# A transformer kernel of two blocks: attention probabilities turned on VectorE and through DRAM instead of on TensorE

## The chip, the cores and the metric

One NeuronCore of a Trainium2 chip runs the whole program. The metric is the time of one execution in device microseconds, taken as the median of three runs. A core has TensorE (matrix products into PSUM), VectorE (DVE in the profile), ScalarE (ACT), GpSimd (POOL), the sync engine (SP), whose queue issues nearly all DMAs here, and 16 DMA engines. All data is float32; products of the large weights are made of three products of rounded parts (fp32r).

## The reference

A sequence of 256 positions with 1024 features goes through two layers. The change is in the second one, in its "forgetting attention": 16 heads of 64 features, causal, in blocks of 128 queries, with a bias of cumulated gate logarithms. Its output is gated with that of another branch.

```
def forgetting_attention(q, k, v, f_pre, q_g, k_g):
    ...
    F = jnp.moveaxis(jnp.cumsum(jax.nn.log_sigmoid(f_pre.astype(f32)), axis=1), 1, 2)
    ...
        logits = jnp.einsum('bhqd,bhkd->bhqk', q_blk, k).astype(f32) * scale + (F_blk[..., :, None] - F[..., None, :])
        logits = jnp.where(k_pos[None, :] <= q_pos[:, None], logits, -jnp.inf)
        p = jax.nn.softmax(logits, axis=-1)
        return jnp.einsum('bhqk,bhkd->bhqd', p.astype(v.dtype), v)
    ...
    merged = jax.nn.sigmoid(g_a) * (y_a @ w_branch_a) + jax.nn.sigmoid(g_b) * (y_b @ w_branch_b)
    x = x + g2 * (merged @ w_out)
```

For the last product TensorE needs the probabilities with the keys on the partitions, while the softmax leaves them with the queries on the partitions: each 128x128 block must be turned.

## The kernel before, in words

The layers are a row of large products (blocks), each of units of two 128-row slices of a weight and 512 columns. A unit is loaded by SP into one of four raw buffers, rounded by ScalarE (`whi`, L1595), and VectorE makes the remainder (`wlo`, L1983). TensorE then runs a half unit for each of the two tiles of 128 positions: six matmuls of 512 columns (L1319, L1323, L1324). The prepared halves stand in five buffers, six from the second branch product on.

Everything else is fitted between the half units. A planner (`plan`, from the top of `build`) writes one list, `order`, which all engines follow. Each side job is a generator that puts its next segment into the list and yields a number of ticks; the numbers are in the table `LAG`. One tick passes behind a half unit, but several in the blocks of `PACED`: `("pace", "gb0")` is 4, `("pace", "gb1")` 9. A call of `drain` lets ticks pass without half units, so that the side jobs stand densely there. Every engine takes its own part of a segment, in the order of the list, and waits on semaphores.

Around the change the blocks are o0, o1 (output gate), ga0, ga1 (gate of branch a), then a drain until `yT` (the turned output of the first branch) is done, then ba0, ba1 (branch product a), gb0, gb1, a drain, bb0, bb1. The jobs of the attention are, for each half of the heads (`fx0`, `fx1`, eight heads each):

- `job_scores`: four rounds. In each, TensorE makes the scores of four heads (L1414), VectorE scales them and adds the bias NF into a buffer of P (L2205, 256 keys for the late queries, 128 for the early ones, which come second), and ScalarE takes the exponential (L1754). P_f is a ring of three buffers of 512 columns.
- `job_weigh`: for i = 0 to 7 (two heads each) TensorE transposes four or two 128x128 blocks of P into a PSUM bank (L1439). VectorE (even i, L2247) or ScalarE (odd i, L1777) copies them to PT_f, a ring of two. One step later TensorE weighs the values with them, PT as stationary operand, fV with 64 columns as moving one (L1458). Each of these float32 products is two records in the trace. After i = 3 and i = 7 VectorE divides the bank by the sums of the exponentials into W1 (L2262, L2267). For `fx0` the end of the first such group waits until `yT` is done, since W1 still holds its input.

Another way of turning is in use elsewhere in the kernel: VectorE turns all 32x32 blocks of a tile in place (L2344, L2509), SP stores the result to the scratch tensor `scr_u` in DRAM (L2713, L2731) and fetches it in another order (L2719, L2738), which puts the blocks where a full transposition has them. The FFN's hidden units (tiles `blocked`, `land_m`, `land_f`) and the queries and keys of this attention (`gate`, which is `gates[0]`, and `land_h`) go that way. `land_h` takes the place of the two buffers PT_f, which are used later. The row `gates[1]` is loaded for the residual behind this stage (`gate_row(1)`).

## Time and profile before

| | |
|---|---|
| median of 3 runs | 945.15 us (944.30 to 945.33) |
| profiled execution, its own time | 944.73 us |
| its span in the trace | 943.4 us |
| TensorE matmuls, busy | 935.1 us, 99% |
| TensorE weight loads, busy | 772.3 us, 82% |
| VectorE, busy | 718.6 us, 76% |
| ScalarE, busy | 509.9 us, 54% |
| granted TensorE clock | 0.999 |
| moved by DMA | 240.31 MB, 255 GB/s on average |

The page gives for each engine the time in which it ran an instruction, and the same in slices of the span. Matmuls are pipelined and their ends are modelled: a duration of 390 ns stands for a matmul that is followed by the next after 230. The distance between starts, or the chain of waits, which charges each piece with the time until the next, tells what a matmul costs. A wait is counted only where an engine had nothing to do, and is put down to what released it.

### The profile page before, as it was taken

How to read it: one execution, taken by the hardware profiler on the slowest of the kernel's cores; microseconds unless marked ns; L12 is line 12 of the kernel's file. 1: busy time of each engine (PE TensorE's matmuls, PEld its weight loads, DVE VectorE, ACT ScalarE, POOL GpSimd, SP SyncE). 2: the span in 40 equal slices, each digit the busy share in tenths (PEclk: the TensorE clock that was granted, in tenths of full speed). 3: DMA queues.
4: the chain of work that ended last, by engine and by line, in shares of the span. 5: the costliest groups of instructions: out<-in, count | busy, mean ns of one | idle time of the engine just before them, and what ended most of it. 6: DMA issues, size and time to landing. Idle time of an engine off the chain costs nothing.

```text
span 943.4 us, 12244 instructions
## 1 busy us (share of the span) xinstructions
PE 935.1 (99%) x4426; PEld 772.3 (82%) x4426; DVE 718.6 (76%) x1090; ACT 509.9 (54%) x792; POOL 50.1 (5%) x58
## 2 busy tenths in 40 slices
PE   9999999999999999999999999999999999999998
PEld 7878788888887888888888888878788888888886
DVE  6897689998676888777769999788666765566662
ACT  6686665564446445454576565456464574544440
POOL 2410000000000000000000121110000000000000
PEclk9999999999999999999999999999999999999999
DMA  9840779999894989998747889984735647666870
GB/s 341 266 152 23 246 245 372 389 387 371 286 317 148 332 326 343 320 345 299 274 133 259 279 281 283 302 338 147 234 125 188 213 137 264 225 223 223 300 234 23
DMA packets 123130, 240.31 MB, mean 255 GB/s; under 512 B 9346, under 2 KB 28954, under 8 KB 122814
## 3 DMA queue, kind: packets, MB, share of 16 engines
q1 hardware_dynamic: 122926, 239.27, 73.8%
q8 instruction: 35, 0.57, 0.2%
q10 hardware_dynamic: 144, 0.27, 0.1%
q14 instruction: 25, 0.20, 0.1%
HBM read 226.35 MB, written 14.20 MB: 255 GB/s over the span
## 4 chain that ended last, share of the span: by engine, by line
PE 87%; DVE 5%; DMA 5%; ACT 1%; issue 1%; SPq 1%; POOL 0%; DVEq 0%; ACTq 0%
PE ps L1319 27%; PE ps L1324 26%; PE ps L1323 26%; DMA raw<-in_w_mix 2%; DVE wlo L1983 2%; PE ps L1458 2%; PE ps L1414 1%; PE ps L1439 1%; PE ps L1350 1%; DMA land_h<-scr_u 1%; PE ps L1372 1%; ACT whi L1595 1%; DMA raw<-in_w_up 1%; DMA raw<-in_w_in 1%; PE ps L1571 1%
## 5 line engine op out<-in xcount | busy, mean ns | idle before, releaser
L1595 ACT ACTIVATE whi<-raw 128x1024 fp32r<-128x1024 f32 (+1 forms) x285 | 294.5, 1046 | 272.6 <-PE ps L1324 169.5
L1983 DVE TENSOR_TENSOR wlo<-raw,whi 128x1024 fp32r<-128x1024 f32 (+1 forms) x285 | 338.4, 1203 | 106.3 <-ACT whi L1595 105.8
L1319 PE MATMUL ps<-whi,hTh 128*128 128x512 f32 (+1 forms) x760 | 300.0, 395 | 0.2 <-DVE nat L2129 0.2
L1324 PE MATMUL ps<-whi,hTl 128*128 128x512 f32 (+1 forms) x760 | 294.4, 387 | 0.0
L1323 PE MATMUL ps<-wlo,hTh 128*128 128x512 f32 (+1 forms) x760 | 294.3, 387 | 0.0
L1319 PEld LDWEIGHTS ps<-whi,hTh 128*128 128x128 f32 x760 | 142.9, 188 | 30.8 <-issue 2.5
L1324 PEld LDWEIGHTS ps<-whi,hTl 128*128 128x128 f32 x760 | 142.7, 188 | 29.5
L1323 PEld LDWEIGHTS ps<-wlo,hTh 128*128 128x128 f32 x760 | 142.9, 188 | 27.8
L2325 DVE CUSTOM_DVE_ANT_0 araw<-araw,crow,colp 128x1024 f32<-128x1024 f32 x72 | 91.9, 1277 | 0.1
L2594 POOL TENSOR_TENSOR stat<-stat,mhalf 128x8 f32<-128x8 f32 (+3 forms) x29 | 36.2, 1260 | 586.0 <-DVE stat L1999 460.3
L1319 PE MATMUL ps<-whi,uh_ffn 128*128 128x512 f32 x164 | 63.9, 390 | 0.0
L1324 PE MATMUL ps<-whi,ul_ffn 128*128 128x512 f32 x164 | 63.8, 389 | 0.0
L1323 PE MATMUL ps<-wlo,uh_ffn 128*128 128x512 f32 x164 | 63.8, 389 | 0.0
L1319 PE MATMUL ps<-whi,uh 128*128 128x512 f32 x128 | 49.9, 390 | 0.0
L1323 PE MATMUL ps<-wlo,uh 128*128 128x512 f32 x128 | 49.8, 389 | 0.0
L1324 PE MATMUL ps<-whi,ul 128*128 128x512 f32 x128 | 49.8, 389 | 0.0
L2374 DVE TENSOR_TENSOR nat<-ps,nat 128x512 f32<-128x512 f32 (+1 forms) x24 | 15.4, 646 | 29.7 <-PE ps L1324 22.3
L1319 PEld LDWEIGHTS ps<-whi,uh_ffn 128*128 128x128 f32 x164 | 30.8, 188 | 6.4
L1324 PEld LDWEIGHTS ps<-whi,ul_ffn 128*128 128x128 f32 x164 | 30.8, 188 | 6.4
L1323 PEld LDWEIGHTS ps<-wlo,uh_ffn 128*128 128x128 f32 x164 | 30.8, 188 | 6.3
L1324 PEld LDWEIGHTS ps<-whi,ul 128*128 128x128 f32 x128 | 24.0, 188 | 5.0
L1323 PEld LDWEIGHTS ps<-wlo,uh 128*128 128x128 f32 x128 | 24.0, 188 | 5.0
(276 smaller groups left out, 1129.2 us busy)
## 6 DMA issues: line engine op xcount, KB each, us to landing
raw<-in_ffn_w_in SPq DMA_DIRECT2D x80, 512.0 KB, 5.1
araw<-in_w_mod SPq DMA_DIRECT2D x72, 512.0 KB, 5.6
raw<-in_w_mix SPq DMA_DIRECT2D x64, 512.0 KB, 4.9
raw<-in_ffn_w_out SPq DMA_DIRECT2D x44, 512.0 KB, 4.9
raw<-in_w_up SPq DMA_DIRECT2D x32, 512.0 KB, 5.4
raw<-in_w_down SPq DMA_DIRECT2D x32, 512.0 KB, 5.3
scr_u<-blocked SPq DMA_DIRECT2D x18, 512.0 KB, 5.0
raw<-in_w_out SPq DMA_DIRECT2D x16, 512.0 KB, 4.3
```

What stands on the lines that cost most here:

```text
L1319: pe.e.matmul(o, ah, h[:, j, :], start=s0, stop=False, skip_group_check=True)
L1323: pe.e.matmul(o, ah, l[:, j, :], start=False, stop=False, skip_group_check=True)
L1324: r = pe.e.matmul(o, al, h[:, j, :], start=False, stop=s1, skip_group_check=True)
L1350: r = pe.e.transpose(bank[:, c * 128:(c + 1) * 128], src[:, (4 * p + c) * 128:(4 * p + c + 1) * 128], ident[:, :])
L1372: r = pe.e.transpose(bank[:, c * 256 + t * 128:c * 256 + t * 128 + 128], src[t][:, (2 * p + c) * 128:(2 * p + c + 1) * 128], ident[:, :])
L1414: return pe.e.matmul(bank[:, c * w:(c + 1) * w], Q[rows, hp + c, ts], K[rows, kc(c), 0:w], start=True, stop=True)
L1458: r = pe.e.matmul(ob[:, h * 64:(h + 1) * 64], buf[:, (nk * c + k) * 128:(nk * c + k + 1) * 128], (fV if a["fox"] else VA)[:, k, v0:v0 + 64 ...
L1595: act.e.activation(uflat(whi, u), uflat(raw, u), ACT.Copy).then_inc(hi.up(u), 1)
L1983: v.tensor_tensor(uflat(wlo, u), uflat(raw, u), uflat(whi, u).bitcast(f32), SUB).then_inc(lo_dve.up(u), 1)
L2325: v.tensor_tensor_reduce(out=w, in0=w, in1=crow[:, :], scale=1.0, scalar=col("bada", 8 * m + i), op0=MUL, op1=ADD, accum_out=to).then_inc( ...
L2374: v.tensor_tensor(b[:, 0:n], pair_of(key)[t][:, c:512], b[:, 0:n], MUL).then_inc(glu.up(name, t), 1)
L2594: g.tensor_tensor(o, a, mhalf[:, 0:n], ALU.pow).then_inc(rstd.up(*key), 1)
```

## The change

The probabilities of `fx0` and `fx1` are no longer transposed by TensorE. For i = 0 to 3 (four heads each, two buffers of P) `swap` has VectorE transpose the 32x32 blocks of two P buffers into `gates[1]` (`blocked_p`). SP stores it to `scr_u` and fetches it into `land_h` (`shuttle_p`), 1024 columns each for i = 0, 1 and 512 for i = 2, 3. `weigh_blocks` weighs straight from `land_h` with a strided view as stationary operand. There is one buffer before the store and one behind the fetch: a swap waits for the store before it, a fetch for the weighing before it. P becomes a ring of four, two of P_f and two halves of `gates[0]`. VectorE waits ahead of the first scores for the jobs that used these buffers. The copies to PT_f and the PSUM banks for the turned blocks go. The lags of the jobs around are set anew, and the pace of gb1 goes from 9 to 6.

The table of lags, as far as it concerns this attention and the blocks beside it:

```
-       ("fox", "fetch"): 6, ("fox", "put"): 4, ("gate", "ga0"): 15, ("gate", "ga1"): 24, ("gate", "gb0"): 8,
-       ("gate", "gb1"): 11, ("fox", 0): 2, ("fox", 1): 5, ("fox", 2): 5, ("fx0", "wait"): 15, ("fx0s", "round"): 15,
...
+       ("fox", "turn"): 3, ("fox", "fetch"): 6, ("fox", "put"): 4, ("gate", "ga0"): 18, ("gate", "ga1"): 22,
+       ("gate", "gb0"): 16, ("gate", "gb1"): 22, ("fox", 0): 2, ("fox", 1): 5, ("fox", 2): 5, ("fx0", "wait"): 11,
+       ("fx0s", "round"): 15, ("fx0s", "wait"): 9, ("fx0s", 0): 1, ("fx0s", 1): 11, ("fx0s", 2): 30, ("fx0s", 3): 1,
+       ("fx0t", 0): 1, ("fx0t", 1): 11, ("fx0t", 2): 10, ("fx0t", 3): 1, ("fx0w", 0): 2, ("fx0w", 1): 1,
+       ("fx0w", 2): 1, ("fx0w", 3): 11, ("fx1", "wait"): 0, ("fx1s", "round"): 10, ("fx1s", "wait"): 0,
+       ("fx1s", 0): 10, ("fx1s", 1): 5, ("fx1s", 2): 5, ("fx1s", 3): 22, ("fx1t", 0): 1, ("fx1t", 1): 1,
+       ("fx1t", 2): 5, ("fx1t", 3): 11, ("fx1w", 0): 4, ("fx1w", 1): 1, ("fx1w", 2): 2, ("fx1w", 3): 3,
...
+       ("pace", "gb1"): 6, ("pace", "kb"): 1, ("pace", "ob0"): 6, ("pace", "ob1"): 16, ("pace", "qa"): 11,
...
+       ("vb", 0): 2, ("yT", "turn"): 35, ("yb", "turn"): 19, ("yb", "wait"): 10, ("fx0f", 0): 10, ("fx0f", 1): 1,
+       ("fx0f", 2): 6, ("fx0f", 3): 6, ("fx1f", 0): 9, ("fx1f", 1): 8, ("fx1f", 2): 8, ("fx1f", 3): 8}
```

`t` is the lag behind a swap, `w` behind a weighing, `f` behind a fetch. The buffers, the planner's new job and the parts of the engines:

```
-    PT_f = Ring([sb(f"fPT{i}", [128, 512], c=sM) for i in range(2)])
+    land_h = Ring([sb("land_h", [128, 1024], c=sM)])
...
+    blocked_h, blocked_p = Ring([gates[0]]), Ring([gates[1]])
+    P_x = Ring([P_f.bufs[0], P_f.bufs[1], gates[0][:, 0:512], gates[0][:, 512:1024]])
...
+        def job_weigh_blocks(name, ready):
...
+            for i in range(5):
+                if i < 4:
+                    while not {(name, 2 * i), (name, 2 * i + 1)} <= done or None not in blocked_p.held:
+                        yield 1
+                    blocked_p.take(name, i)
...
+                    seg(name)
+                    blocked_p.drop(name, i)
+                    yield lag(f"{name}t", i, 2)
+                if i:
+                    b, last = (i - 1) // 2, i % 2 == 0
+                    while not last and outs() >= OUTS or last and name == "fx0" and "yT" not in done:
+                        yield 1
...
+                    seg(name)
+                    land_h.drop(name, i - 1)
...
+                    yield lag(f"{name}w", i - 1, 2)
+                if i < 4:
+                    while None not in land_h.held:
+                        yield 1
+                    land_h.take(name, i)
+                    seg(name)
+                    yield lag(f"{name}f", i, 6)
```

```
+    def p_columns(name, i):
+        return 512 * attention(name)["chunks"](2 * i) // 2
...
+            def weigh_blocks(i):
+                nk = a["qt"](2 * i) + 1
+                ob = misc.buf(name, "o", i // 2)
+                by_key = land_h.buf(name, i)[:, 0:p_columns(name, i)].rearrange("p (m u k) -> p u k m", m=128, u=2)
...
+                pe.wait_ge(*ld_p(name, i))
...
+                            r = pe.e.matmul(ob[:, h * 64:(h + 1) * 64], by_key[:, u, nk * c + k], fV[:, k, v0:v0 + 64],
+                                            start=(k == 0), stop=(k == nk - 1))
+                r.then_inc(weighed.up(name, i), 1)
+                land_h.give(weighed(name, i), name, i)
...
+                if name == "fx0":
+                    dve.wait_ge(*m_summed(3, 1))
+                    dve.wait_ge(*h_sq(3, 1))
+                    dve.wait_ge(*st_h("fox3"))
...
+            def swap(i):
+                out = blocked_p.buf(name, i)[:, 0:p_columns(name, i)].rearrange("p (g i u k) -> p u g k i", g=4, u=2, i=32)
+                dve.wait_ge(*blocked_p.free(name, i))
+                for u in range(2):
+                    n = 2 * i + u
+                    dve.wait_ge(*p_exp(name, n))
+                    v.transpose(out[:, u], P.buf(name, n)[:, 0:p_columns(name, i) // 2].rearrange(
+                        "p (k j g) -> p g k j", j=32, g=4)).then_inc(swapped.up(name, n), 1)
+                    P.give(swapped(name, n), name, n)
...
+        def shuttle_p(name):
+            for i in range(5):
+                if i < 4:
+                    r, slot_at = p_columns(name, i), i % 2 * 131072
+                    sp.wait_ge(*swapped(name, 2 * i + 1))
+                    q.dma_start(bass.AP(scrU.tensor, slot_at, [[r, 128], [1, r]]), blocked_p.buf(name, i)[:, 0:r]).then_inc(
+                        st_p.up(name, i), 16)
+                    blocked_p.give(st_p(name, i), name, i)
+                    yield
+                if i:
+                    yield
+                if i < 4:
+                    sp.wait_ge(*st_p(name, i))
+                    sp.wait_ge(*land_h.free(name, i))
+                    q.dma_start(land_h.buf(name, i)[:, 0:r].rearrange("p (a x) -> p a x", a=4),
+                                bass.AP(scrU.tensor, slot_at, [[r // 4, 128], [32 * r, 4], [1, r // 4]])).then_inc(
+                                    ld_p.up(name, i), 16)
+                    yield
...
+            if g == 1:
+                sp.wait_ge(*st_p("fx1", 3))
```

## Rows read from the trace of the kernel before

**Rows 1.** The page: busy time of the engines over the whole span.

```profile
PE 935.1 (99%) x4426; PEld 772.3 (82%) x4426; DVE 718.6 (76%) x1090; ACT 509.9 (54%) x792; POOL 50.1 (5%) x58
```

**Rows 2.** Busy time by stage, 626 to 712 us; last columns granted clock, DMA share, GB/s.

```profile
626.00:646.00 20.00, 19.40 (x102) 15.55 (x103) 19.73 (x38) 14.40 (x33) 2.91 (x2) 1.00 0.69 236
646.00:661.00 15.00, 14.99 (x98) 12.89 (x97) 12.09 (x27) 9.48 (x21) 0.00 (x0) 1.00 0.31 105
661.00:677.00 16.00, 16.00 (x80) 12.82 (x80) 10.46 (x18) 8.34 (x15) 0.00 (x0) 1.00 0.71 225
677.00:712.00 35.00, 35.00 (x211) 29.24 (x210) 20.45 (x49) 18.02 (x42) 1.61 (x1) 1.00 0.45 151
```

**Rows 3.** The tiles fP and fPT: count, duration ns min/median/max, first and last start.

```profile
L1439 PE MATMUL ps<-ident,fP x48: 270/272/300, 626.6 to 706.5; 128*128 128x128 f32 x48
...
L1458 PEld LDWEIGHTS ps<-fV,fPT x96: 186/192/192, 636.8 to 708.6; 128*128 128x128 f32 x96
...
L2247 DVE COPY fPT<-ps x8: 415/552/690, 629.6 to 704.8; 128x512 f32<-128x512 f32 x4, 128x256 f32<-128x256 f32 x4
L1777 ACT ACTIVATE fPT<-ps x8: 362/480/598, 636.5 to 706.8; 128x512 f32<-128x512 f32 x4, 128x256 f32<-128x256 f32 x4
```

**Rows 4.** The chain that ended last, 600 to 760 us: start, us charged, what.

```profile
637.18 0.84 PE ps L1458 x8
638.02 0.29 PE ps L1319
...
639.46 0.44 PE ps L1439 x4
639.90 0.23 PE ps L1319
...
655.05 0.22 PE ps L1439 x2
...
665.55 1.06 PE ps L1414 x8
```

**Rows 5.** Waits of TensorE, 610 to 760 us: total us, times, longest.

```profile
PE ps L1439 <- ACT fP L1754: 0.7, 1, 0.7
```

**Rows 6.** Tiles gate, blocked and land_f: transposes (ns), DMAs, us to landing.

```profile
L2509 DVE STREAM_TRANSPOSE gate<-nat x8: 665/684/706, 548.7 to 593.0; 128x512 f32<-128x512 f32 x8
L2731 SPq DMA_DIRECT2D scr_u<-gate x4: 338/344/345, 550.1 to 597.7; - x4
...
DMA to landing us min/median/max: 3.0/3.4/4.2
...
L2344 DVE STREAM_TRANSPOSE blocked<-nat x40: 403/670/708, 130.4 to 883.4; 128x512 f32<-128x512 f32 x36, 128x256 f32<-128x256 f32 x4
...
L2719 SPq DMA_DIRECT2D land_f<-scr_u x12: 366/367/977, 324.1 to 893.9; - x12
...
DMA to landing us min/median/max: 4.4/5.1/6.2
```

**Rows 7.** In order of time, VectorE 654 to 662 us and TensorE 660 to 662.

```profile
658.25 3.48 DVE L1983 TENSOR_TENSOR wlo<-raw,whi 128x1024 fp32r<-128x1024 f32 x3
661.66 1.22 DVE L1983 TENSOR_TENSOR late_lo<-raw,late_hi 128x1024 fp32r<-128x1024 f32 x1
...
661.05 0.39 PE L1319 MATMUL ps<-whi,yTh 128*128 128x512 f32 x1
```

**Rows 8.** In order of time around the start of gb0, TensorE and VectorE.

```profile
677.39 0.40 PE L1319 MATMUL ps<-whi,hTh 128*128 128x512 f32 x1
...
678.77 0.55 PE L1458 MATMUL ps<-fV,fPT 128*128 128x64 f32 x4
...
679.74 0.69 DVE L2267 TENSOR_TENSOR W<-ps,stat 128x512 f32<-128x512 f32 x1
681.24 0.69 DVE L2247 COPY fPT<-ps 128x512 f32<-128x512 f32 x1 [0.81 <-PE ps L1439]
```

**Rows 9.** DMA issues, whole span: count, KB each, median us to landing.

```profile
raw<-in_ffn_w_out SPq DMA_DIRECT2D x44, 512.0 KB, 4.9
...
raw<-in_w_branch_b SPq DMA_DIRECT2D x8, 512.0 KB, 3.5
```

More of the change, by code:

```diff
@@ L359, in build @@
     ld_nf = [signal(f"ld_nf{i}", 16) for i in range(2)]
[L361 removed]
+    st_u, st_h, ld_h, st_p, ld_p = (signal(n, 16) for n in ("st_u", "st_h", "ld_h", "st_p", "ld_p"))
     ld_u = [signal(f"ld_u{i}", 16) for i in range(2)]
@@ L2263, in weigh @@
                 dve.wait_ge(*dve_step.now())
-                if a["fox"]:
-                    dve.wait_ge(*turned("yT", 3))
-                    o = W1[:, qt, a["half"] * 512:(a["half"] + 1) * 512]
-                    v.tensor_tensor(heads(o, 8), heads(ob[:, :], 8), bc(r, 8, 64), MUL).then_inc(
-                        yb_put.up(a["half"], qt), 1)
-                    misc.give(yb_put(a["half"], qt), name, "o", i // 4)
-                elif name == "attn_a":
+                if name == "attn_a":
                     v.tensor_tensor(heads(mixed[:, qt, 0:512], 8), heads(ob[:, :], 8), bc(r, 8, 64), MUL).then_inc(
@@ L2278, in weigh, with weighed_heads @@
                     misc.give(mixed_b(qt), name, "o", qt)
+            def swap(i):
+                out = blocked_p.buf(name, i)[:, 0:p_columns(name, i)].rearrange("p (g i u k) -> p u g k i", g=4, u=2, i=32)
+                dve.wait_ge(*blocked_p.free(name, i))
+                for u in range(2):
+                    n = 2 * i + u
[3 more added lines that the diff above has]
+                    P.give(swapped(name, n), name, n)
+            def weighed_heads(i):
+                qt, ob = a["qt"](2 * i), misc.buf(name, "o", i // 2)
+                r, o = st(8, name, "r", qt), W1[:, qt, a["half"] * 512:(a["half"] + 1) * 512]
+                dve.wait_ge(*weighed(name, i))
+                step(v.reciprocal(r, st(8, name, "s", qt)))
+                dve.wait_ge(*dve_step.now())
+                dve.wait_ge(*turned("yT", 3))
+                v.tensor_tensor(heads(o, 8), heads(ob[:, :], 8), bc(r, 8, 64), MUL).then_inc(yb_put.up(a["half"], qt), 1)
+                misc.give(yb_put(a["half"], qt), name, "o", i // 2)
+            if a["fox"]:
+                for i in range(5):
+                    if i < 4:
+                        swap(i)
+                        yield
+                    if i:
+                        if i % 2 == 0:
+                            weighed_heads(i - 1)
+                        yield
+                    if i < 4:
+                        yield
+                return
             n = 4 if name == "attn_b" else 8
@@ L2836, in sync_program @@
             jobs[f"fox{c}"] = shuttle_heads(f"fox{c}")
+        for h in range(2):
+            jobs[f"fx{h}"] = shuttle_p(f"fx{h}")
         for c in range(8):
@@ L2866, in sync_program @@
         sp.wait_ge(*st_h.now())
+        sp.wait_ge(*st_p.now())
     for dry in (True, False):
```

65 lines of the change are left out of this document (42 added, 23 removed), and 13 rows, old and new, of the table LAG.

## The prediction, made before the change was run

> **What bounds the kernel now.** I read the page first. TensorE is busy for 99% of the span, and no other engine is above 82% [rows 1]. Then the table by stage, for the stretch in which the forget-gate attention is weighed (626 to 712 us): TensorE is at 20 of 20, 15 of 15 and 35 of 35 us there except for 0.6 us in the first piece, its clock is granted in full (1.00, the level of 2.4 GHz), and the DMA share is 0.31 to 0.69 [rows 2]. So each microsecond of TensorE's instructions that goes is a microsecond of time, provided that nothing new makes TensorE wait. VectorE is the other thing to read in this table: it is busy 19.73 of 20 us from 626 to 646 [rows 2], and it supplies TensorE with the lower halves of the weights. The kernel is bound by TensorE with VectorE close behind in the first third of the stretch, and with room later.
>
> **What goes from TensorE.** The turned probabilities are 48 transposes [rows 3]. The modelled duration of 272 ns overlaps, so the price comes from the chain: four in a row take 0.44 us, two take 0.22 [rows 4], 0.11 each. 48 x 0.11 = 5.2 us. The weighing matmuls stay: 96 records [rows 3], eight in 0.84 us, so 0.105 each [rows 4]. They are issued in 8 groups where there were 16. The matmul behind such a group is charged 0.29 instead of 0.23 [rows 4], 0.06 x 8 = 0.5 us. The one wait of TensorE in this stretch, 0.7 us until the first exponentials, sits before the first transpose [rows 5]; in the new order two rounds of scores and later blocks stand there instead, and I count 0.7 us as gained. **Gross gain: 5.2 + 0.5 + 0.7 = 6.4 us.** The 16 copies out of PSUM, on VectorE 8 of 0.55 and on ScalarE 8 of 0.48 us [rows 3], were beside TensorE and are worth nothing directly. The third and fourth buffer for probabilities (four now, three before) and the changed lags move work and add none.
>
> **What is added to VectorE, and where it is late.** Eight block transposes of 512 columns and eight of 256. The nearest rows are 684 ns for 512 and 403 (the smallest) for 256 [rows 6]: 8 x 0.68 + 8 x 0.40 = 8.7 us, less 8 x 0.55 = 4.4 us of copies, +4.3 us, of which about half falls before TensorE's unit that is tightest. That unit is the last one of the first branch product: its lower half is the first of three made from 658.25 (so ready at 659.5), and TensorE takes it at 661.05 [rows 7], 1.6 us later. Counting the list of work by the new lags, VectorE gets three pairs of swaps and one more round of scores before that point, and loses its copies; part of this falls into its waits for ScalarE, and I put the lower half 1.4 us later. TensorE has by then lost 20 transposes (2.2 us) and the 0.7 us, and has got one round of scores (1.06 us [rows 4]) that came later before, so it arrives 1.8 us sooner. 1.6 - 1.4 - 1.8 = -1.6: **TensorE waits 1.6 us there.** Bounds: nothing, if VectorE's present waits for ScalarE swallow the swaps, and 3.4 us.
>
> **What the way through DRAM costs.** Store and fetch are issued on SP's queue, and TensorE's weighing waits for the fetch. The store from the gate buffer, the same tile as the new store's neighbour, lands after 3.0/3.4/4.2 us [rows 6]. The fetch's nearest kind is the landing of the FFN blocks, 4.4/5.1/6.2 us [rows 6]. That is with busy queues: loads of 512 KB take 4.9 us there and 3.5 in the gate blocks [rows 9], so I scale 5.1 by the same ratio and take 3.7. The bounds are 3.5 and 6.2 us. The list by the new lags (a half unit is six matmuls, 1.39 us; the blocks gb0 and gb1 count 4 and 6 ticks for each half unit) gives the distance of each weighing from what it needs:
> - First half of the heads: weighing 0 is over ten half units behind its fetch. Weighing 1 has 4.4 us of work between (two rounds of scores, three turns of yT, a half unit) for a fetch of 3.7. Weighings 2 and 3 have 7 and 6 half units. Nothing waits.
> - Second half, weighing 0: swap 0 stands behind the third half unit of gb0. VectorE comes free for it between 679.7 and 681.2, where it scales the first half's output and then waits 0.81 us for TensorE [rows 8]; I take 679.7. Swap to 681.0, store to 684.5, fetch to 688.2. TensorE begins gb0 at 677.39 [rows 8]; six half units (8.4), a round of scores (1.06 [rows 4]) and one turn (0.44) later it is 687.3. It waits 0.9 us.
> - Weighing 1 has four half units and a weighing: no wait. Weighing 2: swap 2 ends 0.5 us before weighing 1 begins, store +3.4, fetch +3.7, so 6.6 us after weighing 1 began; TensorE has 1.7 + 3 x 1.39 + 0.44 = 6.3 us. It waits 0.3. Weighing 3: the fetch needs the only landing buffer, so it goes out behind weighing 2, and only two half units (2.8 us) stand between: 0.2 + 3.7 - 2.8 = 1.1 us.
> Sum 0.9 + 0.3 + 1.1 = **2.3 us of waits**, at the bounds 1.5 (3.0 and 3.5) and 11.4 (4.2 and 6.2). Behind SP's waits for the store stand the weight loads. They are cheap in the gate blocks: of the four lower halves made from 658.25 to 662.88 [rows 7], each serves 2.77 us (12 matmuls of 0.23), which puts VectorE 9 us ahead of TensorE by then. Before the branch products the lead is what the tight unit shows, and the first fetch falls there in a stretch with DMA share 0.69 [rows 2]; I put that in the 1.6 us above. On VectorE each swap waits for the store before it, with lower halves of weights queued behind it; its new waits ahead of the first scores (the fourth fox store, the chunkwise part) are for things that ended some 15 us before, and the wait of the second gate row is for a store of the attention that lies well before it. The 6 MB through DRAM in some 80 us are 75 GB/s on top of 105 to 236 [rows 2].
>
> **The sum.** 6.4 - 1.6 - 2.3 = 2.5 us less. The profiled execution took 944.73 us with a span of 943.4; its successor would be at 942.2. The median of the runs is 945.15, 0.42 above that execution, so the forecast is 942.7 us.
>
> **A strided operand.** The landed block is read as stationary operand with a step of 8 elements (32 bytes) for the late queries and 4 (16 bytes) for the early ones, and VectorE reads the probabilities with a step of 4. No row of before shows either: all stationary loads there are contiguous, and the loads of the weighing take 192 ns at a spacing of 105 [rows 3, 4]. Bounds: nothing, since a spacing of 0.105 for 128 columns is slower than the 0.23 for 512 moving columns and so leaves room for a slower read; and a doubled spacing, 96 x 0.105 = 10.1 us. I take nothing. The Trainium skill (Advanced Engine Details and Errata, SBUF Cachelines) speaks against the change here: it states lines of 16 bytes, full speed when successive reads hit the same line, at least two of them, and a penalty for a new line with each read. By that rule the upper bound would be nearer; no row here shows it.
>
> **The rivals.**
> - *All hidden.* VectorE swallows its swaps in its waits, and the landings are as quick as 3.0 and 3.5 us. For it: the DMA share of 0.31 and 0.45 in the later pieces [rows 2], and ready weights there. Against it: the two half units before weighing 3. Gain 4.9 to 6.4 us: 938.8 to 940.3.
> - *The landings are those of the FFN.* At 5.1 us for the fetch the waits of the second half are 2.3 + 1.7 + 2.5 = 6.5 us, and the sum is 6.4 - 1.6 - 6.5 = -1.7: 946.9 us. At 6.2 and 4.2 it is 951.8. It decides from a fetch of about 4.5 us, where the change is worth nothing. For it: no landing from this scratch tensor was under 4.4 us as one transfer [rows 6]. Against it: the quick loads of the same blocks [rows 9].
> - *The strided load is slow.* This is the case on the other side by one mechanism: 96 loads, place the weighing groups, price up to 10.1 us, of which 1.6 lies in the wait at the tight unit. 945.15 - 2.5 + 8.5 = 951.2 us. The change is worth nothing from a spacing of 0.13 us and is slower by over 0.2% from 0.15.
> - *TensorE's transposes are not worth their spacing*, so that others fill their place: then 1 to 2 us of the 5.2 go, which the range holds.
>
> **How the numbers follow.** Forecast as worked out, 940.5 to 945.5 us: 0.41. All hidden: 0.26. Slow landings: 0.17. Strided load: 0.16. About 0.2% (1.9 us) is what a measurement of this kernel can tell from no change; the borders are 943.3 and 947.0. The forecast's case gives 0.21 faster and 0.20 within. All hidden is faster. Slow landings give 0.04 within and 0.13 slower, the strided load 0.01 and 0.15; with 0.02 of the forecast's case going to slower this is 0.46 faster, 0.24 within, 0.30 slower. The range leaves out a tenth on either side: 938.8 to 951.0.
>
> **What would show it right or wrong.** No transposes of fP on TensorE and 96 loads of land_h; their spacing in the chain (0.105 or more) decides the strided case. TensorE's waits by what released them: DMA land_h behind the weighing, 2.3 us in all, the largest at weighing 3 or 0 of the second half, in the last two gate blocks; DVE wlo, 1.6 us in the branch products. The block transposes at 684 and 403 ns. The store's and the fetch's landing. The granted clock at 1.00: a wait long enough to lose it would cost more than its own length, and that would make the prediction wrong, as would a wait in the first half of the heads, where I count none.

## The result and the profile after

The changed kernel takes **961.05 us** (median of 4 runs, 957.84 to 963.36), where the kernel before took 945.24 in the same session (944.3 to 945.79): ratio 1.0161, 95% interval 1.0136 to 1.0187. It is slower by 1.6%; the forecast was 942.7 us and the range ended at 951.0. The profiled execution took 962.37 us with a span of 961.1, 17.7 us more than the span of before.

The first thing is the page of the kernel after, busy time by engine; it answers [rows 1].

```profile
PE 947.2 (99%) x4378; PEld 783.9 (82%) x4378; DVE 724.6 (75%) x1098; ACT 507.8 (53%) x784; POOL 47.8 (5%) x58
```

TensorE has 48 instructions fewer and is busy 12.1 us longer. So the time has not gone mainly to waits: something that TensorE does has become slower. The table by stage of the kernel after says where (columns as in [rows 2]: the stretch, its length, TensorE, its weight loads, VectorE, ScalarE, GpSimd, then granted clock, DMA share, GB/s).

```profile
626.00:646.00 20.00, 17.41 (x74) 13.60 (x73) 17.19 (x30) 13.71 (x33) 2.07 (x2) 0.91 0.84 293
646.00:661.00 15.00, 14.36 (x73) 12.34 (x72) 11.24 (x30) 10.67 (x27) 0.00 (x0) 0.89 0.74 251
661.00:677.00 16.00, 16.00 (x74) 13.45 (x73) 13.07 (x20) 5.51 (x6) 0.00 (x0) 1.00 0.59 187
677.00:712.00 35.00, 33.78 (x151) 28.48 (x151) 21.69 (x46) 14.03 (x33) 1.09 (x1) 0.90 0.65 212
712.00:735.00 23.00, 23.00 (x100) 20.02 (x101) 11.86 (x17) 8.84 (x12) 0.00 (x0) 0.93 0.40 133
```

Two columns differ from before. TensorE idles 2.6, 0.6 and 1.2 us in three of the stretches. And the granted clock, 1.00 in every stretch before, is 0.91, 0.89, 0.90 and 0.93: parts of them run at the lower level of 1.2 GHz. Length times what is missing from 1.00 gives 1.8 + 1.7 + 3.5 + 1.6 = 8.6 us of TensorE's time at most that the clock took.

The weighing itself, in the view of the tile land_h (duration in ns min/median/max, first and last start) and in the chain that ended last (start, us charged, what), with a matmul of 512 columns at the lower clock as the last line; these answer [rows 3] and [rows 4].

```profile
L1504 PEld LDWEIGHTS ps<-fV,land_h x96: 308/334/336, 648.6 to 727.5; 128*128 128x128 f32 x96
...
648.92 3.75 PE ps L1504 x16
...
659.61 3.63 PE ps L1504 x16
...
686.88 1.69 PE ps L1504 x8
...
699.98 4.03 PE ps L1504 x16
...
704.98 0.43 PE ps L1356
```

A load of the landed block takes 334 ns where a load of the copied block took 192. The chain charges 16 records with 3.63 or 3.75 us and 8 with 1.69, so 0.21 to 0.23 each; before it was 0.84 for eight, 0.105 each. 96 x (0.225 - 0.105) = 11.5 us. The two steps of the read, 32 bytes for the late queries and 16 for the early ones, cost about the same. The group from 699.98 runs for its second half at the lower clock (the clock falls at 701.6 us) and its records still start 0.24 us apart, where the matmul of 512 columns behind it goes from 0.23 to 0.43. So these 2.2 us of strided weighings lose nothing by the clock, and 7.5 us is the better estimate for it.

VectorE's swaps (tile gate, ns min/median/max) and the waits of TensorE from 600 to 760 us (total us, times, longest), after; they answer [rows 6] and [rows 5].

```profile
L2342 DVE STREAM_TRANSPOSE gate<-fP x8: 605/878/1192, 628.8 to 710.1; 128x512 f32<-128x512 f32 x4, 128x256 f32<-128x256 f32 x4
```

```profile
PE ps L1351 <- DVE wlo L2041: 2.6, 1, 2.6
PE ps L1504 <- DVE stat L2263: 1.2, 1, 1.2
PE ps L1446 <- issue: 0.6, 1, 0.6
```

A swap takes up to 1.19 us for 512 columns and from 0.60 for 256, against the 0.68 and 0.40 that I had used. The largest wait is for a lower half of the weights. The wait of 1.2 us stands before the first weighing of the second half of the heads, at 699.98 us. The profile puts it down to VectorE, whose instruction was the last to end before it, but the weighing also waits for its block from DRAM. The fetch, in SP's queue (start, us, what) and in the view of its line in that stretch:

```profile
695.56 0.38 SPq L2846 DMA_DIRECT2D land_h<-scr_u  x1
...
DMA to landing us min/median/max: 4.3/4.3/4.3
```

It lands at 699.84. In the kernels below that keep the order and have no way through DRAM, TensorE doesn't wait at this place, so this wait is the landing's. In order of time on VectorE (start, us, what, and in brackets its idle time before it):

```profile
628.81 2.13 DVE L2342 STREAM_TRANSPOSE gate<-fP 128x512 f32<-128x512 f32 x2 [3.02 <-ACT fP L1810]
630.84 1.17 DVE L2041 TENSOR_TENSOR wlo<-raw,whi 128x1024 fp32r<-128x1024 f32 x1
```

VectorE stands 3.02 us in front of the first swap until ScalarE has the exponentials, then swaps for 2.1 us, and only then makes the lower half that TensorE has been waiting for. In before such a wait for the exponentials stood on TensorE, 0.7 us [rows 5], and the lower halves went past it.

**The account**, from these rows: 48 transposes and eight groups gone, -5.7; weighings slower, +11.5; waits, 4.4 for 0.7, +3.7; clock, at most +8.6. Sum +18.1 us, or 17.0 with 7.5 for the clock, against the 17.7 of the spans. The sum fits, but it doesn't tell which part of the change brings the waits and the half clock. The experiments do.

### The profile page after: what moved, and what is told of

Same layout as the page of the kernel before. It is cut to its first block, busy times and chain, and to the rows that moved or that the text cites. A ratio compares the mean times of both kernels' runs of the same rounds, so it can differ in the third digit from the quotient of the medians.

```text
span 961.1 us, 12168 instructions
## 1 busy us (share of the span) xinstructions
PE 947.2 (99%) x4378; PEld 783.9 (82%) x4378; DVE 724.6 (75%) x1098; ACT 507.8 (53%) x784; POOL 47.8 (5%) x58
## 4 chain that ended last, share of the span: by engine, by line
PE 86%; DVE 6%; DMA 5%; ACT 1%; issue 1%; SPq 0%; POOL 0%; DVEq 0%; ACTq 0%
PE ps L1351 27%; PE ps L1355 26%; PE ps L1356 26%; DMA raw<-in_w_mix 3%; PE ps L1504 2%; DVE wlo L2041 2%; PE ps L1446 1%; PE ps L1404 1%; DMA land_h<-scr_u 1%; PE ps L1382 1%; ACT whi L1651 1%; PE ps L1486 1%; DMA raw<-in_ffn_w_in 1%; DMA raw<-in_w_in 0%; PE ps L1471 0%
```

## Experiments

Each ran in three rounds or more beside the kernel before on the same chip, where nothing else is said. The kernel before had medians of 944.29 to 945.52 us beside them, so ratios are to be compared, and differences between two kernels are given from their ratios (1% is 9.45 us). A kernel that leaves a part out, or reads other elements than it should, doesn't give the reference's output; it only prices that part. Those that give it are called complete. **Theory S**, after reading the traces: the strided reads are the loss. **Rival**, Theory W in the expectations: the way through DRAM and its waits are.

### TensorE's operand packed

```
-  by_key = land_h...rearrange("p (m u k) -> p u k m", m=128, u=2)
+  by_key = land_h...rearrange("p (u k m) -> p u k m", m=128, u=2)
```

VectorE's swap stays as it was, strided in its read and in its write.

> The changed kernel with one line different: the landed block is read as stationary operand in packed rows of 128 elements instead of with a step of 8 or 4 (the output is then built from other elements of the block, and so is not the reference's). Theory S (the strided stationary operand is the cost, directly and by the clock): the weighing loads go from a spacing of about 0.23 us back to 0.105, which is 12 us of TensorE, and the low stretches of the granted clock behind a weighing go with them (three of four, 13.7 us at half rate, some 6.8 us); 941 to 946 us. Theory W (waits for the way through DRAM and for VectorE are the cost, and the clock falls because of them): the loads may get quicker but TensorE then waits for the landings instead; 953 us or more.

Measured: **954.7 us** (950.82 to 955.77), ratio 1.0101, 1.0078 to 1.0125. That is 5.7 us less than the changed kernel (6.4 by the medians), and not the 15 or more that I had expected. TensorE's waits of this kernel, 600 to 760 us:

```profile
PE ps L1446 <- issue: 4.0, 1, 4.0
PE ps L1504 <- DMA land_h<-scr_u: 3.3, 2, 1.9
```

The weighings are back at a spacing of 0.11 us, but 7.3 us of waits stand where the changed kernel had 4.4: TensorE arrives sooner and meets VectorE's queue and the landings. The 4.0 us have no releaser in the profile. The scores that wait need the banks that the scaling of earlier scores (L2263) frees, and VectorE's order shows when it got there:

```profile
647.60 0.67 DVE L2045 TENSOR_TENSOR yTl<-ps,yTh 128x512 fp32r<-128x512 f32 x1
648.19 1.14 DVE L2342 STREAM_TRANSPOSE gate<-fP 128x256 f32<-128x256 f32 x2
649.24 0.24 DVE L2263 CUSTOM_DVE_ANT_0 gate<-ps,NF 128x128 f32<-128x128 f32 x1
```

VectorE has no gap here from 642 to 650 us; TensorE starts its scores at 649.80, 0.1 us after VectorE is through with the second of the four (in the changed kernel 653.95 and 653.85). Theory S was incomplete.

### The stride alone, in the kernel before

```
+  if a["fox"]:
+      kept = buf[:, 0:nk * 256].rearrange("p (m j) -> p j m", j=2 * nk)[:, nk * c + k]
```

> The kernel before with the stationary operand of the attention's weighing read with a step of 4 elements (16 bytes, 64 of the records) or 2 elements (8 bytes, 32 records), from the same tile fPT (other elements of it, so the output is not the reference's). Nothing of the way through DRAM is in it. Theory S: the 64 records go to a spacing of about 0.22 us, +7.4 us, the 32 stay at 0.105 if 8 bytes are free or add 3.7 us; the clock may fall behind the groups; 952 to 962 us. Rival L (the loads are slow because the tile has just been landed or is written by DMAs meanwhile, not for the step): 945 us, spacing 0.105.

Measured: **952.74 us** (952.22 to 953.4), ratio 1.0090, 1.0074 to 1.0107. 64 of the records have a step of 16 bytes and 32 one of 8. The tile fPT, and a row of the table by stage:

```profile
L1461 PEld LDWEIGHTS ps<-fV,fPT x96: 193/329/332, 636.9 to 716.1; 128*128 128x128 f32 x96
...
646.00:661.00 15.00, 14.99 (x86) 13.44 (x85) 10.29 (x27) 9.34 (x22) 0.00 (x0) 1.00 0.31 107
```

No wait from 600 to 760 us, no loss of clock there, and 8.4 us more (7.5 by the spans). In the trace eight weighings with a step of 16 bytes start 0.233 us apart, and those with a step of 8 bytes 0.117, near the packed 0.111. So the step of two elements costs next to nothing and the step of four doubles the load: 64 x 0.12 = 7.7 us. The price of the stride is TensorE's own, with nothing else of the change about.

### VectorE's swap packed

```
-  "p (k j g) -> p g k j", j=32, g=4)       (read)
+  "p (k g j) -> p g k j", j=32, g=4)
-  "p (g i u k) -> p u g k i"               (write)
+  "p (g u k i) -> p u g k i"
```

> The changed kernel with VectorE's block transposes reading and writing packed runs of 32 (other elements, so the output is not the reference's), TensorE still reading with the steps of the change. The swaps go from 1.19 and 0.60 us to 0.68 and 0.40, 5.7 us of VectorE in all. Theory S: VectorE's part is beside TensorE except where a lower half stands behind it; 958 to 961 us. Theory W: VectorE's swaps are what makes TensorE late, and 4 us or more go: 957 us or less.

Measured: **956.8 us** (955.25 to 960.68), ratio 1.0137, 1.0112 to 1.0162: 2.3 us less than the changed kernel by the ratios (4.3 by the medians). With intervals of 2.4 us on either side of both kernels that is not clear of noise. In its trace TensorE's waits fall from 4.4 to 1.6 us.

### Both packed

> Leaves out: the right order of the keys (both VectorE's swap and TensorE's read run over packed elements; the output is not the reference's). The way through DRAM is as in the changed kernel. Theory W: e1_packed_view took 6.4 us off by TensorE's operand and e4_swap_packed 4.3 us by VectorE's; if the two costs are separate they add: 961.05 - 6.4 - 4.3 = 950.4, range 948.5 to 951.5, and TensorE's waits on landings stay, with half clock behind them. Rival (the two overlap: with TensorE quicker VectorE's time is hidden, or what it saves is given back as a wait on the landing): 953 to 955, no better than e1_packed_view. If the way through DRAM is free once both strides are gone: 941 to 945.

Measured: **947.02 us** (944.99 to 952.26), ratio 1.0030, 1.0012 to 1.0049. The two edits alone bring 5.7 and 2.3 us, together 12.4. More than the sum, it seems, though the excess of 4.4 us is about as large as the noise of four ratios. TensorE's waits and its swap's duration in this kernel:

```profile
PE ps L1446 <- issue: 3.1, 1, 3.1
PE ps L1504 <- DMA land_h<-scr_u: 1.4, 2, 0.7
PE ps L1351 <- DVE wlo L2041: 0.7, 1, 0.7
...
L2342 DVE STREAM_TRANSPOSE gate<-fP x8: 402/557/711, 626.7 to 699.0; 128x512 f32<-128x512 f32 x4, 128x256 f32<-128x256 f32 x4
```

Packed, the swap is at 0.71 and 0.40 us, which is what [rows 6] had shown. The kernel with four fetches for one, below, has the write packed and the read not:

```profile
L2342 DVE STREAM_TRANSPOSE gate<-fP x8: 584/844/1098, 627.7 to 709.1; 128x512 f32<-128x512 f32 x4, 128x256 f32<-128x256 f32 x4
```

It takes up to 1.10 us where the swap with both strided took 1.19. So most of the price is the read with a step of four elements, and some 0.1 us is the write's.

### The way through DRAM left out

The swaps write gates[1] and the landing buffer in turns, and TensorE weighs from there:

```
-  pe.wait_ge(*ld_p(name, i))
+  pe.wait_ge(*swapped(name, 2 * i + 1))
```

First with TensorE's operand packed, as above:

> Leaves out: the store to DRAM and the fetch back, so TensorE weighs what VectorE's swap left in SBUF (not the probabilities' transpose; the output is not the reference's). TensorE's operand is packed as in e1_packed_view (954.7 us there); two buffers take turns. Theory W (what is left of the loss after the packing is TensorE's waits and the half clock that follows each): the two waits on the landings (1.9 + 1.4 us) and the half clock behind them (two stretches of 3.4 us, half of each lost, 3.4 us) go: 954.7 - 6.7 = 948.0, range 946.5 to 950; the 4.0 us wait behind VectorE's queue at 646 us stays. Rival V (the way through DRAM costs nothing here, the loss is VectorE's queue alone, and another wait takes the place of those on the landings): 952.5 to 955.5.

Measured: **945.71 us** (943.94 to 948.2), ratio 1.0010, 0.9998 to 1.0022. From 1.0101 that is 8.6 us for the way through DRAM, more than the 6.7 of waits and clock that I had counted. Then with both strided reads kept:

> Leaves out: the store to DRAM and the fetch back, as in e5_packed_no_way; both strided reads stay as in the changed kernel (961.05 us). The output is not the reference's. Theory W: in the changed kernel no wait of TensorE over 0.5 us stands against a landing (the slow weighings give the fetches the time), so the way through DRAM is worth only little here: 957.5 to 961. Rival (the way through DRAM is the main loss): 950 to 955. With e5_packed_no_way it gives the price of the strided operand without the way: I expect 961 - 948 = about 10 us or more, near the 12 us that the 96 records' spacing grew by; below 7 us would say that half of the spacing is covered elsewhere.

Measured: **958.79 us**, ratio 1.0138, 1.0117 to 1.0158; one of its four executions took 3599 us and is not in the ratio (the median of the other three is 958.03). By the ratios it is 2.2 us less than the changed kernel, which is not clear of noise (the difference is uncertain by 3 us). So the way through DRAM is worth some 2 us or nothing where TensorE is slow and 8.6 where it is quick, and 3.8 where both reads are packed (1.0030 against 0.9990, the kernel further down). The strided operand is worth 12.1 us where the way is left out and 5.7 where it is there. They cover each other. The kernel was run once more for its trace, below.

### What is left when neither is there

Without the way, packed for TensorE, the kernel is still 7 us above the 938.5 that the removal promised (944.9 less 6.4). TensorE's waits in that kernel, and its stretch from 646 us:

```profile
PE ps L1452 <- issue: 4.0, 1, 4.0
...
646.00:661.00 15.00, 10.97 (x60) 9.10 (x59) 11.20 (x35) 9.74 (x27) 0.00 (x0) 0.77 0.32 106
```

4.0 us of waiting and at most 15 x 0.23 = 3.4 us of clock, part of which falls into the wait: up to 7.4 us. Either the new order of the work is at fault or the swaps in VectorE's queue are. First the order, by one number that puts the scores behind the drain:

```
-  ("fx1s", "wait"): 0
+  ("fx1s", "wait"): 126
```

> e5_packed_no_way (945.71 us; the way through DRAM left out, TensorE's operand packed, output not the reference's) with one number of the order changed: the first scores of the second half of the heads (fx1) are put off until after the drain at 646 us, where TensorE waited 4.0 us for VectorE there and then ran 6.8 us at the half clock. Nothing else differs but the place of that one group. Theory W (a wait costs its length and then half of the half-clock stretch behind it): 945.7 - 4.0 - 3.4 = 938.3 us, range 937.5 to 941; that is the time before less the 6.4 us that I had for the 48 transposes and the eight groups. Rival G (the gross gain was never there, and the 4 us wait is another form of work that TensorE would have to wait for anyway): 944 to 946.

Measured: **946.18 us** (944.29 to 947.46), ratio 1.0018, 1.0009 to 1.0028. A miss. The two largest waits of TensorE:

```profile
PE ps L1410 <- DVE yTl L2051: 2.6, 1, 2.6
PE ps L1357 <- DVE wlo L2047: 1.5, 1, 1.5
```

The wait went over to the turns of yT that now stand first, and a stretch at half clock of the same length stands there too. Then the swaps:

```
-  v.transpose(out[:, u], P.buf(name, n)[:, 0:p_columns(name, i) // 2]...)
+  v.transpose(gates[1][:, 32 columns of their own], P.buf(name, n)[:, 0:32])
```

> Leaves out the way through DRAM and nearly the whole swap: VectorE turns 32 columns for each tile in place of 512 or 256, TensorE weighs packed values that are not the probabilities (output not the reference's). So what is left of the change is what it removes: 48 transposes, eight groups, the copies out of PSUM. The order of the work is that of the changed kernel. Theory Q (the waits at 628 and at 646 us, which e9_no_way_later moved but did not remove, are VectorE's queue, made late by the swaps): the wait at 646 falls from 4.0 us to under 1 and with it the half clock behind it: 937.5 to 940.5, the time before less 4 to 7 us. Rival O (the wait at 646 us comes from the order written for the change, whatever VectorE has to do): 944 to 946, as e5_packed_no_way.

Measured: **940.96 us** (938.82 to 942.94), ratio 0.9960, 0.9944 to 0.9976: the first kernel of the study that is faster than before. With the swaps at full size but packed:

> Leaves out the way through DRAM; the swap is there at full size but packed on both sides (0.70 us for a full tile in e6_all_packed, 1.19 us in the changed kernel), TensorE's operand is packed too; output not the reference's. Theory Q: the wait at 646 us shortens from 4.0 us (e5_packed_no_way) to about the 3.1 us of e6_all_packed, and the half-clock stretch behind it stays: 943.5 to 945.5. If the swap's stride is the main thing on VectorE: 940 to 942.

Measured: **944.21 us** (940.23 to 945.33), ratio 0.9990, 0.9976 to 1.0003. The waits and the stretch from 646 us, of the kernel without swaps and, after the three dots, of that with packed swaps:

```profile
PE ps L1452 <- DVE yTl L2051: 1.2, 1, 1.2
...
646.00:661.00 15.00, 14.31 (x79) 11.83 (x80) 12.14 (x31) 8.70 (x24) 0.00 (x0) 1.00 0.30 100
```

```profile
PE ps L1452 <- issue: 2.9, 1, 2.9
...
646.00:661.00 15.00, 12.10 (x73) 10.17 (x73) 11.43 (x35) 11.40 (x28) 0.00 (x0) 0.89 0.36 117
```

It is VectorE's queue. With the order unchanged and the swaps nearly gone, the wait shrinks to 1.2 us and the clock stays at 1.00.

### Where the half clock comes from

> The kernel of e8_strided_no_way again (958.79 us), for its trace. The question is the half clock: in the changed kernel one of the four stretches at half clock (715 us) stands behind no wait of TensorE over 0.6 us, but amid a group of 16 slow weighings. Theory W (a stretch at half clock comes behind a wait): none is found without a wait of about 1 us or more within some 5 us ahead. Rival L (a group of 16 slow weighings alone brings it): stretches stand at the four places where 16 slow weighings are, waits or not. Time 957 to 960 us.

Measured once: **956.94 us**. TensorE's wait after 640 us, its groups of slow weighings in order of time (start, us, what), and its table by stage in pieces around two of them:

```profile
PE ps L1452 <- issue: 1.5, 1, 1.5
...
656.88 3.79 PE L1510 MATMUL ps<-fV,land_h 128*128 128x64 f32 x16
...
696.11 4.07 PE L1510 MATMUL ps<-fV,gate 128*128 128x64 f32 x16
...
706.84 3.84 PE L1510 MATMUL ps<-fV,land_h 128*128 128x64 f32 x16
...
660.00:664.00 4.00, 4.00 (x19) 3.39 (x20) 3.90 (x8) 1.79 (x2) 0.00 (x0) 1.00 0.01 1
696.00:699.00 3.00, 3.00 (x16) 2.89 (x13) 2.87 (x11) 1.82 (x10) 0.00 (x0) 1.00 0.40 153
699.00:703.00 4.00, 4.00 (x13) 3.38 (x14) 0.12 (x1) 0.94 (x1) 0.00 (x0) 0.57 0.61 197
...
709.00:713.00 4.00, 4.00 (x15) 3.65 (x16) 1.69 (x4) 1.43 (x2) 0.00 (x0) 0.58 0.24 90
```

The last wait is over by 651 us, and TensorE is busy 4.00 of 4.00 us where its mean clock is 0.57 and 0.58. So "behind a wait only" is wrong. Both stretches begin as a group of 16 slow weighings ends. Behind the group at 656.9 the clock stays at 1.00. In the changed kernel it is three of four groups too, though two of the three have a wait beside them (1.2 us ahead, 0.6 behind). No group of 8 did it there, nor in the kernel before with its strided reads. The kernel with the six numbers of the order moved (below) shows it once more without a wait: TensorE waits last at 704.85 us, a group of 16 slow weighings runs from 717.21 to 720.81, and then

```profile
721.00:724.00 3.00, 3.00 (x9) 2.33 (x9) 2.92 (x5) 0.25 (x1) 0.00 (x0) 0.50 0.29 87
```

In all five traces with such groups, 12 of the 17 have the clock fall during the group or within 1.3 us of its end, and in 8 of these 12 TensorE waits nowhere (0.2 us or more) from 9 us before the group until the clock falls. The kernel without swaps has four groups of 16 packed weighings, and its clock stays at 1.00 through all of them. The next kernel cuts the groups by a piece of GEMM work between the halves:

```
-  weigh_blocks(i - 1)                      (16 records)
+  weigh_blocks(i - 1, (0,)); yield; weigh_blocks(i - 1, (1,))
```

> Complete. The changed kernel (961.05 us), strided reads and all, but the four groups of 16 slow weighings are cut into eight groups of 8, with GEMM work between the halves of each; the late queries' groups of 8 stay. In the changed kernel three of the four groups of 16 (at 648.8, 700.0 and 711.5 us) are followed or overlapped by a stretch at half clock (653.8, 701.6 and 715.3 us, 13.7 us in all), the fourth is not, and no group of 8 is, there or in e3_before_strided. Theory L (16 slow weighings in a row bring the half clock): those three stretches go and 6.8 us with them, less about 0.3 us for four more groups: 954 to 956 us, and the clock stays at 1.00 outside what follows TensorE's wait at 629 us. Rival C (the share of slow loads in a longer time counts, or chance): 959 to 962, with stretches at half clock still there.

Measured: **966.65 us** (964.4 to 968.43), ratio 1.0219, 1.0190 to 1.0248. It missed, by the waits that the cut brought:

```profile
PE ps L1507 <- DMA land_h<-scr_u: 5.6, 2, 4.1
PE ps L1354 <- DVE wlo L2048: 2.6, 1, 2.6
```

The waits come to 10.8 us for 4.4. The largest, 4.1 us, stands before the first weighing of the second half: the store behind its swap landed 4.9 us after its issue, where it took 2.7 in the changed kernel. Why that store was slower isn't shown. As to the clock, it stayed up behind two of the three groups that were cut; at the third a wait of 4.1 us stood, and there it fell, as it did behind waits of 1.5 and 1.0 us around the last group of 8. And it fell (0.77 from 646 to 661 us) at the end of the group in the drain, which the order had left in one piece, before TensorE waited there. That fits "16 in a row", but the clock is not the only thing that the cut changed, and why 5 of the 17 groups bring no half clock stays open.

### Can it be mended?

A form in which TensorE reads its operand as four runs of 32 queries gave no time, so nothing is known of it. Here the DMA engines do the packing, with four fetches for one, in runs of 128 bytes, then of 256 (both kernels are complete):

```
+  for b in range(4):
+      q.dma_start(land_h...rearrange("p (x a i) -> p a x i", a=4, i=32)[:, b],
+                  bass.AP(scrU.tensor, slot_at + 32 * r * b, [[r // 4, 128], [32, r // 128], [1, 32]]))
```

> Complete and right in what it computes: the DMA engines do the packing. The fetch is four DMAs for each pair of tiles, in runs of 32 elements (128 bytes) where it was one in runs of 64 to 256, and lands in the order in which TensorE reads packed. Theory W: TensorE's 96 weighings are at 0.11 us as in e1_packed_view; the fetches take longer to land than 3.6 us (8 times the descriptors: I guess 5 to 8 us), so the waits on the landings grow by 1 to 3 us each at two to four places: 955 to 962. If the DMA engines take the short runs in their stride: 954 to 955.5, equal to e1_packed_view, and better than the changed kernel by 6 us.

Measured: **956.05 us** (955.81 to 957.86), ratio 1.0121, 1.0105 to 1.0136.

> Complete. A compromise between the changed kernel and e7_packed_by_dma: the fetch moves runs of 64 elements (256 bytes), four DMAs, and TensorE's weights stand 8 bytes apart. In e3_before_strided such a step gave 0.117 us between weighings, against 0.233 at 16 bytes and 0.111 packed, so TensorE pays about 0.6 us for all 96. VectorE's swap still reads at a step of 16 bytes (1.19 us). Theory W: landings are shorter than in e7_packed_by_dma (TensorE waited 6.7 us on four of them there) by half of the descriptors: 950 to 955 us. Rival (the number of DMAs, four for one, makes the landing late, and not their runs): as e7_packed_by_dma, 955.5 to 957.

Measured: **956.19 us** (955.81 to 959.21), ratio 1.0132, 1.0115 to 1.0150. The fetches of the latter, and TensorE's waits for them:

```profile
L2847 SPq DMA_DIRECT2D land_h<-scr_u x32: 524/612/1087, 632.2 to 716.3; - x32
...
DMA to landing us min/median/max: 2.2/2.8/5.1
...
PE ps L1504 <- DMA land_h<-scr_u: 4.4, 2, 2.8
```

Each of the four fetches lands 2.8 us after its issue; what is late is the last of four, since each takes SP 0.61 us to issue where the one fetch took 0.37. Both forms end level, 3 to 4 us below the changed kernel by the ratios (5 by the medians) and 11 to 12 above the one before. The last two move six numbers of the order, on the form with runs of 256 bytes and on the changed kernel itself:

```
-  ("fx0", "wait"): 11, ("fx1s", "wait"): 0, ("fx1f", 0..3): 9, 8, 8, 8
+  ("fx0", "wait"): 15, ("fx1s", "wait"): 126, ("fx1f", 0..3): 14, 12, 12, 12
```

> Complete. e10_runs_of_64 with six numbers of the order changed: the first scores of fx1 after the drain as in e9_no_way_later, the first swap four slots later (so that VectorE does not stand in front of it for the exponentials), and 3 to 5 more slots between fetch and weighing in the second half. Theory W: the waits at 628, 646 and in the second half shrink, each with its half-clock stretch: 943 to 949, which would be level with the kernel before, not better than it by more than 0.2%. Rival (the slots push the second half so late that what comes after waits): 950 to 956.

Measured: **966.96 us** (965.31 to 969.85), ratio 1.0242, 1.0219 to 1.0266.

> Complete. The changed kernel with both strided reads and the one fetch, and the six numbers of e11_runs_of_64_later. It asks how much of the 16 us is order and how much stride. Theory W: the strided weighings alone cost TensorE 12 us of spacing; what the order can give back are the waits (2.6 + 1.2 + 0.6 us) and the half-clock stretches that follow waits, some 3 to 7 us: 953 to 958. Rival (order is the main thing): 948 or less. Rival (clock falls also behind the slow weighings alone, whatever the waits): 957 to 961, with half-clock stretches still there in the profile.

Measured: **972.11 us** (971.92 to 972.61), ratio 1.0295, 1.0278 to 1.0313. The largest waits of TensorE, 600 to 760 us, and from VectorE's order of time the swap ahead of the second of them:

```profile
PE ps L1504 <- DMA land_h<-scr_u: 4.6, 2, 2.6
PE ps L1404 <- DVE stat L2263: 3.5, 1, 3.5
...
655.15 1.16 DVE L2342 STREAM_TRANSPOSE gate<-fP 128x256 f32<-128x256 f32 x2 [3.06 <-DMA scr_u<-gate]
```

In both, every theory missed by over 10 us. With the later first swap VectorE's swaps come into the drain at 650 us, where TensorE has nothing but scores and turns to do. There a swap stands for 3.06 us until the store of the swap before it has landed, since both use the one buffer, and the scaling of the scores behind it is late: this is what TensorE waits 3.5 us for. The landings wait as before. The six numbers were moved together, so their shares aren't known. Neither kernel tells how much a good order could save; I found no complete version that is faster than the kernel before.

### The ladder

From the kernel before, in ratios to it, each step one edit:

| kernel | ratio | step |
|---|---|---|
| transposes and copies gone, hardly any swap, no DRAM | 0.9960 | -0.40% (-3.8 us) |
| swaps at full size, packed | 0.9990 | +0.30% (+2.8 us) |
| the swap reads and writes with a step | 1.0010 | +0.20% (+1.9 us) |
| TensorE reads at a step of four or eight | 1.0138 | +1.28% (+12.1 us) |
| the way through DRAM | 1.0161 | +0.23% (+2.2 us) |

A step is uncertain by 0.2 to 0.3%, so the two of 0.2% are hardly told from nothing; the 1.28% is clear. The steps depend on their order: taken ahead of TensorE's stride, the way costs 0.9% (1.0101 against 1.0010), and the stride then 0.6%.

## Why the prediction was wrong, step by step

- **Gross gain, 6.4 us.** Right in kind. With the transposes gone and hardly any swap the span is 937.9 us, 5.5 below before, with 1.4 us of waits of TensorE left in it; that execution is one of the faster of six, and the ratio gives 3.8.
- **"A strided operand ... I take nothing."** This is the step that failed. The bounds were 0 and 10.1 us, and the truth was beyond the upper one: 0.105 became 0.21 to 0.23, so 11.5 us by the chain and 12.1 in the ladder. The reason for nothing was that a spacing of 0.105 left room for a slower read. It leaves none: as the load went from 192 to 334 ns, the spacing went from 0.111 to 0.238 us. The Trainium skill (Advanced Engine Details and Errata, SBUF Cachelines) states a penalty where each read meets a new line of 16 bytes. The traces agree: the step of 8 bytes, two reads to a line, is nearly free (0.117 against 0.111) and that of 16 costs double (0.233). The rival of the strided load is thus the mechanism that came about, but I had priced it at 951.2 us, without the clock and without VectorE's own strided read.
- **Swaps at 684 and 403 ns, +4.3 us net.** 1.19 and 0.60: 8 x 1.19 + 8 x 0.60 = 14.3 us for 8.7. The rows that I took read contiguously. I had weighed a price of the step for TensorE and didn't ask the same of VectorE, which reads with a step of 16 bytes. Packed, the rows' prices held (up to 0.71, and 0.40).
- **"TensorE waits 1.6 us" at the last unit of the first branch product.** The mechanism, VectorE late with what TensorE needs, was right, and the place wrong. TensorE waits at 629 us for a lower half (2.6 us) and around 650 for VectorE (0.6, and 4.0 once its own loads are quick), and not at all in the branch product. The row for it was there: VectorE busy 19.73 of 20 us from 626 to 646 [rows 2]. And I didn't list what stands behind the wait for the exponentials, once it is VectorE that waits: the lower halves.
- **The way through DRAM, 2.3 us of waits in the second half.** Right in price: the fetch was taken at 3.7 us and the store at 3.4.

```profile
L2846 SPq DMA_DIRECT2D land_h<-scr_u x8: 359/372/1013, 633.7 to 723.3; - x8
...
DMA to landing us min/median/max: 2.6/4.1/5.6
```

  The tile's fetch lands after 4.1 us, the store after 2.0/3.5/5.6. With packed reads TensorE waits 1.4 us for landings (both packed) or 3.3 (its operand alone), at weighings 0 and 3 of the second half, as written. In the changed kernel weighing 0 waits 1.2 us for its landing, where 0.9 was forecast, and the slow weighings hide the rest.
- **The granted clock at 1.00.** Wrong, by 7.5 to 8.6 us. The text named the danger, a wait long enough to lose it, and counted no wait as such; in the sum it had no term. The other source, slow loads in a row, was not in the text at all. The eight groups in place of 16, which I had booked as a gain of 0.5 us, may be part of it: only the groups of 16 were followed by it without a wait.
- **The sum.** By the measured terms: 6.4 gained, less 11.5 (stride), 4.4 (waits in place of 1.6 + 2.3) and up to 8.6 (clock) is up to 18.1 us slower. The range ended at 951.0 because the strided rival stood alone in it, with its bound as its end; the cases of a slow load, a late VectorE and a lost clock were set against one another, and here they came together.

## What to carry to other kernels

Before a transpose or a copy is taken away, look at which engine now reads the data in its old order, and price the read by its step: at fp32, a step of two elements was nearly free here and one of four doubled TensorE's spacing and made most of the rise of VectorE's transpose from 0.71 to 1.19 us. Where an engine is busy 19.7 of 20 us and feeds the one that bounds the kernel, what is put on it can come onto the path, as the swaps did here, and any wait of it holds what is queued behind. And a loss on a bound engine is no single term: waits and slow loads brought stretches at half clock with them, some 8 us on top of 15.

## What the runs showed of the hardware

- A TensorE weight load of 128 x 128 fp32 takes 192 ns packed, 329 at a step of 16 bytes and 334 at one of 32; weighings with 64 columns stand 0.111, 0.117, 0.233 and 0.238 us apart at steps of 4, 8, 16 and 32 bytes. Twice the step beyond 16 bytes costs next to nothing more.
- At the lower clock packed weighings stood 0.213 us apart instead of 0.111 (the kernel with four fetches, 16 of them from 699.2 us), strided ones 0.24 as at the higher.
- VectorE's 32x32 block transpose of 512 columns takes up to 0.71 us with read and write packed, 1.10 with the read at a step of 16 bytes and the write packed, and 1.19 with the write strided too.
- TensorE's clock fell to its lower level with TensorE busy 4.00 of 4.00 us and no wait for 48 us, at the end of 16 slow weighings in a row. With TensorE's operand packed, or at a step of 8 bytes, every stretch at half clock between 620 and 730 us stood in or behind a wait, of 1.4 to 4.0 us in the kernels whose order is that of the change, though not every such wait brought one (none at 1.5 us where the first scores were put off).
- The fetch cut in four takes SP 0.61 us for each issue where the one fetch takes 0.37, so the last of the four is later than the one, though each lands sooner after its issue (2.8 against 4.1 us).
